# A trunk layer with 16 experts: router chain reordered, expert columns gathered directly, output projection tile by tile

## The chip, the cores and the metric

One core of a Trainium2 chip runs the whole kernel. The metric is device time in microseconds of one execution; the figure for a kernel is the median of its runs, and a profile is one further execution.

## The reference

One layer over 384 tokens of width 1024: 128 context tokens and 256 latent ones (`T` = 3 tiles of 128).

```
h   = LN0(x) * (1 + scale1) + shift1
x   = LN1(alpha * x + gate1 * (merged @ w_out))       # merged: two mixing branches, each projected and gated
h2  = LN0(x) * (1 + scale2) + shift2
aff = softmax(h2 @ w_router)                          # 16 experts, context and latent tokens apart
gate, idx = top_k(aff.T, cap)                         # each expert takes 16 context and 32 latent tokens
xe  = h2[idx];  hid = silu(xe @ w_gate) * (xe @ w_up) # per expert 1024 x 2816, twice
out[idx] += (hid @ w_down) * gate                     # 2816 x 1024
x   = LN2(alpha * x + gate2 * out)
```

All in fp32. The expert weights are 34.6 MB for each of the 16 experts.

## The kernel before

Semaphores and the order in each engine's program are written out by hand. Tiles of 128 tokens come in `ORDER` (1, 2, 0): latent, latent, context.

*Projections.* Every weight matrix comes in chunks of 512 columns (2 MB, `WCHUNKS`; 16 and 17 are `pa`, 18 and 19 `pb`, 20 and 21 the output projection `wo`). A chunk is split into a rounded part (ScalarE, `split_high`) and a rest (VectorE, `split`); a job of PE (`job`, L740) makes one 128 x 512 result from three products over 8 k-tiles, so 24 matmuls, into PSUM bank 0 or 1, and waits until the result of the job before the last is copied. Chunks alternate between two pairs of slots at the top of the ring: one pair is free when the chunk two before has been used. A `pa` or `pb` result is multiplied by its gate and added to `merged`; a `wo` result is multiplied by the gate row `g1b` and added to alpha * x (L1396, L1397). Six `wo` jobs, in order (tile, half) = (0,0), (1,0), (0,1), (1,1), (2,0), (2,1). Merged tiles are turned by PE (L696) before they are used.

*Between.* VectorE makes both layer norms of a tile (`layer_norms`: statistics L1363, affine L1370 and L1372, first part of h2 L1705); ScalarE scales (L1314) and GpSimd adds the shift (L670) for the first two tiles, VectorE does all of it for the third. h2 lies row by row. PE turns it, ScalarE copies it, PE makes the router logits (L966), softmax follows, the probabilities are turned and copied to SBUF, and VectorE finds the best 8 at a time (`best`, L1717 to L1721): four rounds for latent, two for context tokens. The slots go to DRAM and back, to be broadcast to 128 partitions (L677, L679). The selection of expert 0 is made another way, from a turned comparison (L1757, L1004, L1759). The broadcasts of rows (gate, scale, shift, norms) are DMAs on GpSimd's queue; `bc_loaded` counts ten.

*Experts.* Per expert PE gathers the 64 rows by a one-hot product (L1021, 512 wide), ScalarE copies, PE turns them (L1026), VectorE copies, then gate and up (L1038, 192 instructions in the trace), the turn of the hidden part (L1046), down (L1060), the combination (L1068), which VectorE adds to x (L1794). SyncE's queue loads the weights into a ring of six quarters (gate and up in 4 quarters of 2.88 MB each, down in 4 groups): the first two quarters after the merged tiles are copied, the next after the last `wo` copy, all later ones when PE has used what lay there (`gate_used`, `up_used`, `down_used`).

## Time and profile before

| | |
|---|---|
| median of 3 runs | 1866.29 us (1866.17 to 1867.25) |
| profiled execution | 1867.64 us, of which the span is 1865.8 |
| granted TensorE clock, mean | 0.97 of full speed |
| busy: PE, PEld, DVE, ACT, POOL | 1672.9, 799.4, 503.0, 338.3, 46.3 us |
| read from HBM | 637.8 MB, mean 344 GB/s |

A span runs from the first instruction to the last. The projections end at 543 us, the experts begin at 574 us and fill the rest. PE's busy time is not PE at its peak, and a share of the whole span says nothing of one stage; the stages are read one by one below.

### The profile page before, as it was taken

Reading aid. Unit: us, or ns where it says so; the run is one execution under the profiler, and the core shown is the slowest. Engines: PE = TensorE matmul, PEld = TensorE weight load, DVE = VectorE, ACT = ScalarE, POOL = GpSimd, SP = SyncE. Lnnn points to the kernel's source line nnn. Section 1 sums busy time; section 2 is a strip of 40 time slices with the busy share of each in tenths; the row PEclk is TensorE's granted clock in tenths of the full one; section 3 lists DMA queues with packets and bytes.
Section 4 is the critical chain, followed back from the end, with each engine's and each line's share of the span. In section 5 each row is a group of like instructions: output and inputs, shape, how many; then the busy total and the mean of one; then the engine's idle time right before and its main releaser. Section 6 shows DMA issues by size and latency. Waiting matters only on the chain.

```text
span 1865.8 us, 18738 instructions
## 1 busy us (share of the span) xinstructions
PE 1672.9 (90%) x7753; PEld 799.4 (43%) x7753; DVE 503.0 (27%) x956; ACT 338.3 (18%) x663; POOL 46.3 (2%) x71
## 2 busy tenths in 40 slices
PE   5999999999977998998988999798998989999896
PEld 2767787778763333333333323233333323333232
DVE  5385547775672101011010101101011010101102
ACT  2443355553321000000000000000000000000000
POOL 2001000010010000000000000000000000000000
PEclk9999999999988999999999999999999999999998
DMA  9683343325559999999999999999999999999994
GB/s 355 219 278 98 110 125 90 91 76 182 188 201 376 431 431 429 432 428 431 433 429 430 431 430 430 431 433 428 428 433 429 431 431 431 429 431 429 431 432 184
DMA packets 60569, 642.04 MB, mean 344 GB/s; under 512 B 6142, under 2 KB 6286, under 8 KB 32878
## 3 DMA queue, kind: packets, MB, share of 16 engines
q1 hardware_dynamic: 56464, 629.96, 81.6%
q0 software_dynamic: 4064, 11.54, 1.9%
q8 instruction: 26, 0.43, 0.1%
q14 instruction: 15, 0.12, 0.0%
HBM read 637.77 MB, written 3.71 MB: 344 GB/s over the span
## 4 chain that ended last, share of the span: by engine, by line
PE 67%; DMA 22%; DVE 7%; ACT 2%; issue 2%; POOL 0%; SPq 0%; DVEq 0%; ACTq 0%; POOLq 0%
PE banks L1038 24%; DMA ring<-in_w_exp_down 16%; PE banks L740 15%; PE banks L1060 11%; PE banks L1068 4%; DMA ring<-in_w_exp_up 4%; PE banks L1021 2%; PE banks L738 2%; PE banks L696 1%; PE banks L755 1%; DMA ring<-in_w_in 1%; PE banks L896 1%; DVE O L1786 1%; PE banks L1026 1%; DMA O<-in_ln_b 1%
## 5 line engine op out<-in xcount | busy, mean ns | idle before, releaser
L1038 PE MATMUL banks<-ring,O 128*64 128x512 f32 (+1 forms) x3072 | 641.5, 576 | 27.6 <-DMA ring<-in_w_exp_up 13.8
L1038 PEld LDWEIGHTS banks<-ring,O 128*64 128x64 f32 x3072 | 219.6, 134 | 441.3 <-issue 414.3
L1060 PE MATMUL banks<-ring,O 128*64 128x512 f32 x1408 | 328.3, 623 | 25.1 <-DMA ring<-in_w_exp_down 15.0
L1060 PEld LDWEIGHTS banks<-ring,O 128*64 128x64 f32 x1408 | 101.6, 144 | 242.0 <-issue 195.3
L1781 DVE TENSOR_TENSOR O<-O,banks 128x512 f32<-128x512 f32 (+1 forms) x48 | 28.0, 639 | 650.3 <-PE banks L1038 650.3
L740 PE MATMUL banks<-slot_parts,X_parts 128*128 128x512 f32 x672 | 183.4, 403 | 0.0
L740 PEld LDWEIGHTS banks<-slot_parts,X_parts 128*128 128x128 f32 x672 | 121.3, 188 | 39.5 <-issue 11.0
L1786 DVE TENSOR_TENSOR O<-banks,O 128x512 f32<-128x512 f32 x32 | 20.6, 687 | 390.1 <-PE banks L1060 390.1
L740 PE MATMUL banks<-slot_parts,H_parts 128*128 128x512 f32 x432 | 115.7, 396 | 0.4 <-DVE X L1397 0.4
L1463 DVE TENSOR_TENSOR slot_parts<-ring,slot_parts 128x512 fp32r<-128x512 f32 x176 | 110.2, 687 | 16.6 <-ACT slot_parts L1107 15.8
L1068 PE MATMUL banks<-O 128*128 128x512 f32 x192 | 86.6, 601 | 22.4 <-DVE O L1786 22.4
L1330 ACT ACTIVATE O<-banks 128x512 f32<-128x512 f32 x16 | 9.6, 597 | 469.8 <-PE banks L1021 469.8
L740 PEld LDWEIGHTS banks<-slot_parts,H_parts 128*128 128x128 f32 x432 | 82.0, 191 | 17.9 <-DVE X L1397 0.9
L1336 ACT ACTIVATE O<-banks 128x512 f32<-128x512 f32 (+1 forms) x48 | 24.3, 559 | 355.0 <-PE banks L1046 354.8
L1107 ACT ACTIVATE slot_parts<-ring 128x512 fp32r<-128x512 f32 x144 | 77.8, 620 | 56.2 <-DMA ring<-in_w_proj_b 19.1
L1333 ACT ACTIVATE O<-banks 128x512 f32<-128x512 f32 (+1 forms) x48 | 23.5, 562 | 327.6 <-PE banks L1038 327.6
L1794 DVE TENSOR_TENSOR X<-X,banks 128x512 f32<-128x512 f32 x90 | 61.8, 687 | 31.1 <-PE banks L1068 31.1
L1068 PEld LDWEIGHTS banks<-O 128*128 128x128 f32 x192 | 35.2, 190 | 74.7 <-issue 40.6
L1021 PE MATMUL banks<-O 128*64 128x512 f32 x192 | 46.1, 617 | 12.4 <-DVE X L1794 11.8
L1046 PE MATMUL banks<-kf,O 128*128 128x128 f32 x176 | 28.4, 315 | 31.1 <-DVE O L1781 31.1
L696 PE MATMUL banks<-kf,O 128*128 128x128 f32 x144 | 26.6, 315 | 23.0 <-DVE O L1421 11.2
L1046 PEld LDWEIGHTS banks<-kf,O 128*128 128x128 f32 x176 | 24.3, 214 | 42.4 <-DVE O L1781 42.4
(252 smaller groups left out, 1070.7 us busy)
## 6 DMA issues: line engine op xcount, KB each, us to landing
ring<-in_w_exp_gate SPq DMA_DIRECT2D x64, 2816.0 KB, 30.6
ring<-in_w_exp_up SPq DMA_DIRECT2D x64, 2816.0 KB, 26.1
ring<-in_w_exp_down SPq DMA_DIRECT2D x32, 3072.0 KB, 23.5
ring<-in_w_exp_down SPq DMA_DIRECT2D x16, 4096.0 KB, 28.0
ring<-in_w_in SPq DMA_DIRECT2D x16, 2048.0 KB, 9.9
ring<-in_w_mod SPq DMA_DIRECT2D x16, 1024.0 KB, 10.8
ring<-in_w_exp_down SPq DMA_DIRECT2D x16, 1024.0 KB, 32.3
O<-in_w_mod SPq DMA_DIRECT2D x8, 1024.0 KB, 5.3
```

What stands on the lines that cost most here:

```text
L696: x = pe.transpose(banks[:, 2 + b % 2, i * P:(i + 1) * P], src, ident)
L738: x = pe.matmul(out[:, 0:NT], w[:, k, i * P:(i + 1) * P], a[:, k, :], **flags)
L740: x = pe.matmul(out, a[:, k, i * P:(i + 1) * P], w[:, k, :], **flags)
L1021: x = pe.matmul(banks[64 * w:64 * w + 64, 3, :], sel[:, t, :], h2_half(t, w), start=(t == 0), stop=(t == T - 1))
L1038: x = pe.matmul(banks[64 * w:64 * w + 64, 3 * m + b, 0:(i1 - i0) * P], xeT[:, k % 4, 64 * (k // 4):64 * (k // 4) + 64], w4[:, kk, w, i0 * ...
L1046: x = pe.transpose(banks[:, b, (i - i0) * P:(i - i0 + 1) * P], hid_cols[:, i, :], ident)
L1060: x = pe.matmul(banks[64 * w:64 * w + 64, 6 + dc, :], hidT[:, i, 64 * w:64 * w + 64], wd[:, i, w, dc * BANK:(dc + 1) * BANK], start=(i == ...
L1068: pe.matmul(banks[:, 2 * t + dc, :], selT[:, t * P:(t + 1) * P], yrow[:, dc * BANK:(dc + 1) * BANK], start=not last, stop=True, skip_group ...
L1107: return act.activation(out, in_, ACT.Copy, scale=scale)
L1463: dve.tensor_tensor(low[:, k, :], w[:, k, :], high[:, k, :].bitcast(F32), ALU.subtract).then_inc(w_split, 1)
L1786: dve.tensor_tensor(yrow[:, cs], banks[:, 6 + dc, :], g2s[:, cs], ALU.mult).then_inc(y_cp, 1)
L1794: dve.tensor_tensor(dst, dst, banks[:, n, :], ALU.add).then_inc(acc_done, 1)
```

## The change

Five edits. (1) The output projection goes tile by tile; its first chunk has a place of its own below the slots, loaded once `pa` is done, and its second one takes the slots of the first `pb` chunk. The reload of x goes ahead of the `pb` chunks; scale2 is incremented beside `pb`; the last three broadcast rows have a semaphore of their own. (2) h2 is written chunk-wise, each k-tile's 128 columns together (column p * 8 + k of x goes to chunk k), from x, scale and shift read with a step of 8. ScalarE normalises from x, GpSimd multiplies and adds in halves. (3) The chain from h2 to the slots is interleaved, and the top-8 search reads the probabilities in PSUM. (4) Each expert's columns are gathered directly: 24 matmuls with a chunk of h2 as weights and the one-hot selection (32 or 16 slots, both in 32 columns) as moving data; the gathered rows and their turn are gone. (5) The slots are broadcast by PE, for expert 0 first, for all others between gate and up of expert 0, which is now outside the loop; the way by DRAM is gone, and the last norm's two rows are loaded after that broadcast.

```diff
+WO_FIRST, WO_SECOND = (CHUNK_OF["out", h * BANK] for h in range(2))
+PAIR = [n % 2 for n in range(WO_FIRST)] + [2, 0]
...
-WO_ORDER = [(0, 0), (1, 0), (0, 1), (1, 1), (2, 0), (2, 1)]
+WO_ORDER = [(n, h) for n in range(T) for h in range(2)]
...
+        def w_raw(n, k):
+            return wslot[2 * PAIR[n]][:, k, :] if PAIR[n] < 2 else reg(4 * UNIT + k * BANK, BANK)
+
+        def w_low(n, k):
+            if PAIR[n] < 2:
+                return wpart[2 * PAIR[n]][:, k, :]
+            return tile_of(E_r, k) if k < 6 else tile_of(spare_r, k - 6)
+
+        def w_high_of(n, k):
+            if PAIR[n] < 2:
+                return wpart[2 * PAIR[n] + 1][:, k, :]
+            return tile_of(spare_r, k + 2) if k < 2 else tile_of(C_r, k - 2)
...
+        h2_cols = O4[:].rearrange("p (t k n) -> p t k n", t=T, k=KT)
 
         def h2_half(t, w):
-            return h2[:, t, :].rearrange("p (n w k) -> p w n k", w=2, k=4)[:, w]
-
-        xeT = O3[:, BANK:2 * BANK].rearrange("p (i n) -> p i n", n=P)
+            return h2_cols[:, t, 4 * w:4 * w + 4, :]
+
+        def in_columns(row, w):
+            return row.rearrange("p (n k) -> p k n", k=KT)[:, 4 * w:4 * w + 4, :]
@@ sync
             def load_chunk(n):
                 if n < 2:
                     sp.wait_ge(mod0_used, 4 * n + 2)
+                elif n == WO_FIRST:
+                    sp.wait_ge(job_done, J_PA[-1] + 1)
                 else:
-                    sp.wait_ge(low_used, n - 1)
-                sp.dma_start(wslot[low_slot(n)], w_chunk(n)).then_inc(wsem[n % 2], 16)
+                    sp.wait_ge(low_used, before_in_pair(n)[-1] + 1)
+                dst = wslot[2 * PAIR[n]] if PAIR[n] < 2 else reg(4 * UNIT, KT * BANK).rearrange("p (k n) -> p k n", k=KT)
+                sp.dma_start(dst, w_chunk(n)).then_inc(wsem[PAIR[n]], 16)
...
-            for n in range(5, len(WCHUNKS)):
+            for n in range(5, CHUNK_OF["pb", 0]):
                 load_chunk(n)
-
             sp.wait_ge(job_done, J_GB[-1] + 1)
             sp.dma_start(x_r[:, 0, :], x_prompt[0]).then_inc(ld_x2, 16)
             sp.dma_start(x_r[:, 1:3, :], x_sample[0].rearrange("(t p) d -> p t d", p=P)).then_inc(ld_x2, 16)
+            for n in range(CHUNK_OF["pb", 0], len(WCHUNKS)):
+                load_chunk(n)
...
+            def load_quarter(m, q):
+                sp.dma_start(quarter((4 * m + q) % 6), gate_up(m, 0, q)).then_inc((land_g, land_u)[m][q], 16)
+
+            sp.wait_ge(job_done, J_PB[-1] + 1)
+            load_quarter(1, 1)
             wait_family(sp, F_M)
-            for q in range(4):
-                if q == 2:
-                    wait_job_copied(sp, J_WO[-1])
-                sp.dma_start(quarter(q), gate_up(0, 0, q)).then_inc(land_g[q], 16)
-            for q in range(4):
-                if q >= 2:
-                    sp.wait_ge(gate_used, q - 1)
-                sp.dma_start(quarter((4 + q) % 6), gate_up(1, 0, q)).then_inc(land_u[q], 16)
+            load_quarter(0, 0)
+            wait_job_copied(sp, J_WO[-1])
+            for q in range(1, 4):
+                load_quarter(0, q)
+            load_quarter(1, 0)
+            for q in range(2, 4):
+                sp.wait_ge(gate_used, q - 1)
+                load_quarter(1, q)
@@ gpsimd
             for g in range(2):
-                pool.dma_start(sh2b[:, g, :], mods[g, 3:4].to_broadcast((P, D))).then_inc(bc_loaded, 16)
-            pool.dma_start(l1b, ln1_b.to_broadcast((P, D))).then_inc(bc_loaded, 16)
+                pool.dma_start(sh2b[:, g, :], mods[g, 3:4].to_broadcast((P, D))).then_inc(bc_late, 16)
+            pool.dma_start(l1b, ln1_b.to_broadcast((P, D))).then_inc(bc_late, 16)
 
             for n in range(2):
                 t = ORDER[n]
-                if n == 0:
-                    pool.wait_ge(bc_loaded, 160)
+                g = min(t, 1)
                 pool.wait_ge(h2_norm, n + 1)
-                pool.tensor_tensor(h2[:, t, :], h2[:, t, :], sh2b[:, min(t, 1), :], ALU.add).then_inc(h2_ready[n], 1)
+                for w in range(2):
+                    dst = h2_half(t, w)
+                    pool.tensor_tensor(dst, dst, in_columns(sc2b[:, g, :], w), ALU.mult).then_inc(h2_scaled, 1)
+                    pool.wait_ge(h2_scaled, 2 * n + w + 1)
+                    pool.tensor_tensor(dst, dst, in_columns(sh2b[:, g, :], w), ALU.add).then_inc(h2_ready[n], 1)
 
             wait_job_copied(pool, J_WO[-1])
...
-            pool.wait_ge(rt_slots, 1)
-            pool.dma_start(slot_tokens, slots[:, 0:SLOT]).then_inc(rt_stored, 16)
-            pool.wait_ge(rt_stored, 16)
-            pool.dma_start(slot_bc, slot_tokens.rearrange("e s -> (e s)")[None].to_broadcast((P, NE * SLOT))).then_inc(rt_bc, 16)
-
-            pool.wait_ge(rt_tt, 1)
+            pool.wait_ge(rt_all, 1)
             pool.dma_start(l2g, ln2_g.to_broadcast((P, D))).then_inc(ld_end, 16)
             pool.dma_start(l2b, ln2_b.to_broadcast((P, D))).then_inc(ld_end, 16)
@@ tensor
+            for b in range(2):
+                logits(0, b)
+            for n in (1, 2):
+                for b in range(2):
+                    pe.wait_ge(h2_ready[n], b + 1)
+                    turn_half(h2, n, b)
+                    if n == 2 and b:
+                        turn_probs(0)
+                    logits(n, b)
             turn_probs(1)
-            logits(2)
             turn_probs(2)
+            wait_job_copied(pe, J_WO[-1])
+
+            def one_expert(e):
+
+                return ident[0:NE, e:e + 1].to_broadcast((NE, P))
+
+            def gather(k, ts):
+
+                s0 = k % 4 * SLOT + (LAT0 if ts[0] else CTX0)
+                for t in ts:
+                    x = pe.matmul(banks[:, 6 + k // 4, s0:s0 + CAP_L], h2_cols[:, t, k, :], sel[:, t, :],
+                                  start=(t == ts[0]), stop=(t == ts[-1]))
+                return x
+
+            pe.wait_ge(rt_lat, 1)
+            pe.matmul(banks[:, 1, 0:CAP_L], one_expert(0), slots[:, 0:CAP_L], start=True, stop=True).then_inc(rt_first, 1)
+            pe.wait_ge(sel_ready, 2)
+            for k in range(KT):
+                gather(k, (1, 2))
+            pe.wait_ge(rt_ctx, 1)
+            pe.matmul(banks[:, 1, CAP_L:SLOT], one_expert(0), slots[:, CAP_L:SLOT], start=True, stop=True).then_inc(rt_first, 1)
+            pe.wait_ge(sel_ready, 3)
+            for k in range(KT):
+                x = gather(k, (0,))
+            x.then_inc(xet_done, 1)
             pe.wait_ge(rt_slots, 2)
...
+            def broadcast_slots():
+
+                for e in range(NE):
+                    x = pe.matmul(banks[:, 6 + e // 8, e % 8 * SLOT:(e % 8 + 1) * SLOT], one_expert(e), slots[:, 0:SLOT],
+                                  start=True, stop=True)
+                x.then_inc(rt_all, 1)
...
+            def expert(e, first=False, last=False):
+
+                if not first:
+                    pe.wait_ge(sel_ready, e * T + T)
+                    for k in range(KT):
+                        gather(k, (1, 2))
+                        x = gather(k, (0,))
+                    x.then_inc(xet_done, 1)
+                pe.wait_ge(xet_cp, 2 * e + 2)
                 pe.wait_ge(acc_done, e * 6 + 6)
-                for t in range(T):
-                    for w in range(2):
-                        x = pe.matmul(banks[64 * w:64 * w + 64, 3, :], sel[:, t, :], h2_half(t, w),
-                                      start=(t == 0), stop=(t == T - 1))
-                x.then_inc(xe_done, 1)
-                pe.wait_ge(xe_cp, e + 1)
-                for i in range(4):
-                    x = pe.transpose(banks[:, 4, i * P:(i + 1) * P], xe_cols[:, i, :], ident)
-                x.then_inc(xet_done, 1)
-                pe.wait_ge(xet_cp, e + 1)
...
+                    if first and m == 0:
+                        broadcast_slots()
+                        pe.wait_ge(rt_cols, 2)
@@ scalar
+                act.wait_ge(x1_ready, n + 1)
+                act.activation(h2_cols[:, t], x_r[:, t, :].rearrange("p (n k) -> p k n", k=KT), ACT.Identity, scale=s("rstd", t, t + 1),
+                               bias=s("nmr", t, t + 1)).then_inc(h2_norm, 1)
+            for parity in range(2):
+                tile_copy(act, F_H2, 0, h2T, cp, parity)
             x1_dev(2, 0)
+            for parity in range(2):
+                tile_copy(act, F_H2, 1, h2T, cp, parity)
             x1_dev(2, 1)
+            router_exps(0)
+            for parity in range(2):
+                tile_copy(act, F_H2, 2, h2T, cp, parity)
+            router_exps(1)
+            router_exps(2)
+            act.wait_ge(h2_norm, 2)
+            times_alpha(0)
...
-            with act.Fori(0, NE) as e:
-                act.wait_ge(xe_done, e + 1)
-                act.activation(xe, banks[:, 3, :], ACT.Copy).then_inc(xe_cp, 1)
+            act.wait_ge(xet_done, 1)
+            cp(xeT[:, 0:4, :], banks[:, 6, 0:4 * SLOT].rearrange("p (k s) -> p k s", s=SLOT)).then_inc(xet_cp, 1)
+            act.wait_ge(rt_all, 1)
+            for w in range(2):
+                cp(slot_bc[:, 8 * w:8 * w + 8, :], banks[:, 6 + w, :].rearrange("p (e s) -> p e s", s=SLOT)).then_inc(rt_bc, 1)
@@ vector
             for n, j in enumerate(J_PB):
                 job_copy(j)
-                if 0 < n < T:
+                if n == 0:
+                    dve.wait_ge(bc_loaded, 112)
+                    for g in range(2):
+                        note(dve.tensor_scalar(sc2b[:, g, :], sc2b[:, g, :], 1.0, None, ALU.add))
+                elif n < T:
                     split(19, KT // 2 * (n - 1), KT // 2 * n)
-                if T <= n < T + 2:
-                    split(20, KT // 2 * (n - T), KT // 2 * (n - T + 1))
-            merged_low(0)
-            merged_low(1)
-            for k in range(0, KT, 2):
-                split(21, k, k + 2)
-            dve.wait_ge(bc_loaded, 160)
+                elif n == T:
+                    split(20)
+                else:
+                    merged_low(n - T - 1)
+                    split(21, KT // 2 * (n - T - 1), KT // 2 * (n - T))
             dve.wait_ge(ld_x2, 32)
-            for g in range(2):
-                note(dve.tensor_scalar(sc2b[:, g, :], sc2b[:, g, :], 1.0, None, ALU.add))
 
             def softmax_max(n):
                 t = ORDER[n]
...
-                if n == 2:
-                    softmax_max(1)
+                job_copy(between)
...
+                rstd(t)
+                dve.tensor_scalar(s("nmr", t, t + 1), s("mv", 2 * t, 2 * t + 1), s("rstd", t, t + 1), -1.0,
+                                  ALU.mult, ALU.mult).then_inc(x1_ready, 1)
...
             job_copy(J_WO[0])
+            merged_low(2)
             job_copy(J_WO[1])
-            merged_low(2)
-            job_copy(J_WO[2])
-            layer_norms(0)
+            dve.wait_ge(bc_late, 48)
+            layer_norms(0, J_WO[2])
             job_copy(J_WO[3])
-            layer_norms(1)
-            job_copy(J_WO[4])
-            softmax_max(0)
-            softmax_scale(0)
-            job_copy(J_WO[5])
-            layer_norms(2)
-            softmax_scale(1)
-            tile_copy(dve, F_H2, 2, h2T, dve.tensor_copy, 1)
-
+            layer_norms(1, J_WO[4])
             note(dve.memset(slots, -1.0))
             note(dve.memset(gates, 0.0))
-            turned_probs(0)
-            turned_probs(1)
-            best(SEQ, NT, LAT0, CAP_L)
+
+            t = ORDER[2]
+            half_stats(t, 0)
+            job_copy(J_WO[5])
+            stats(t, ws=(1,)).then_inc(x1_var[0], 1)
+            dve.wait_ge(x1_std[0], 3)
+            rstd(t)
+            link(affine(x_r, t, l1g, l1b))
+            stats(t).then_inc(x1_var[1], 1)
+            softmax_max(0)
+            dve.wait_ge(x1_std[1], 3)
+            rstd(t)
+            g = min(t, 1)
+            for w in range(2):
+                dst = h2_half(t, w)
+                link(dve.scalar_tensor_tensor(out=dst, in0=in_columns(x_r[:, t, :], w), scalar=s("mv", 2 * t, 2 * t + 1),
+                                              in1=in_columns(sc2b[:, g, :], w), op0=ALU.subtract, op1=ALU.mult))
+                dve.scalar_tensor_tensor(out=dst, in0=dst, scalar=s("rstd", t, t + 1), in1=in_columns(sh2b[:, g, :], w),
+                                         op0=ALU.mult, op1=ALU.add).then_inc(h2_ready[2], 1)
+            softmax_scale(0)
+            softmax_max(1)
+            softmax_scale(1)
+            dve.wait_ge(rt_tr, 2)
+            best(lat_probs, LAT0, 0, CAP_L // 8)
             softmax_max(2)
+            best(lat_probs, LAT0, 1, CAP_L // 8)
             softmax_scale(2)
-            turned_probs(2)
-            best(0, SEQ, CTX0, CAP_C)
-            settle()
-            note(dve.tensor_scalar(slots[:, LAT0:LAT0 + CAP_L], idxu[:, LAT0:LAT0 + CAP_L], float(SEQ), None, ALU.add))
-            link(dve.tensor_copy(slots[:, CTX0:CTX0 + CAP_C], idxu[:, CTX0:CTX0 + CAP_C]))
+            best(lat_probs, LAT0, 2, CAP_L // 8)
+            best(lat_probs, LAT0, 3, CAP_L // 8)
+            dve.tensor_scalar(slots[:, LAT0:LAT0 + CAP_L], idxu[:, LAT0:LAT0 + CAP_L], float(SEQ), None, ALU.add).then_inc(rt_lat, 1)
+            dve.wait_ge(rt_tr, 3)
+            best(context_probs, CTX0, 0, CAP_C // 8)
+
+            def first_selection(t):
+                s0 = LAT0 if t else CTX0
+                dve.tensor_scalar(sel[:, t, :], banks[:, 1, s0:s0 + CAP_L], iota_c[:, t:t + 1], None, ALU.is_equal).then_inc(sel_ready, 1)
+
+            dve.wait_ge(rt_first, 1)
+            first_selection(1)
+            first_selection(2)
+            best(context_probs, CTX0, 1, CAP_C // 8)
+            dve.tensor_copy(slots[:, CTX0:CTX0 + CAP_C], idxu[:, CTX0:CTX0 + CAP_C]).then_inc(rt_ctx, 1)
+            dve.wait_ge(rt_first, 2)
+            first_selection(0)
+            dve.wait_ge(rt_lat, 1)
+            dve.wait_ge(rt_ctx, 1)
             dve.tensor_copy(slots[:, SLOT:2 * SLOT], slots[:, 0:SLOT]).then_inc(rt_slots, 1)
             dve.tensor_copy(gates[:, SLOT:2 * SLOT], gates[:, 0:SLOT]).then_inc(rt_slots, 1)
+            dve.wait_ge(xet_done, 1)
+            dve.tensor_copy(xeT[:, 4:8, :], banks[:, 7, 0:4 * SLOT].rearrange("p (k s) -> p k s", s=SLOT)).then_inc(xet_cp, 1)
```

## Rows read from the trace of the kernel before

**Rows 1.** The page's part 2: GB/s moved, in 40 equal slices.

```profile
GB/s 355 219 278 98 110 125 90 91 76 182 188 201 376 431 431 429 432 428 431 433 429 430 431 430 430 431 433 428 428 433 429 431 431 431 429 431 429 431 432 184
```

**Rows 2.** The chain of waits in time order: start us, length us, what.

```profile
501.65 11.69 DMA O<-in_ln_b
...
842.50 28.15 DMA ring<-in_w_exp_down
```

**Rows 3.** Windows: stretch and its length, busy us per engine, PEclk, DMA share, GB/s.

```profile
540.00:545.00 5.00, 5.00 (x31) 4.33 (x29) 4.22 (x7) 1.90 (x3) 0.38 (x1) 1.00 0.00 0
...
560.00:565.00 5.00, 4.26 (x21) 4.03 (x19) 3.91 (x15) 0.60 (x1) 0.00 (x0) 0.50 0.93 347
...
585.00:590.00 5.00, 5.00 (x26) 1.64 (x24) 0.00 (x0) 0.00 (x0) 0.00 (x0) 1.00 0.63 221
...
640.00:720.00 80.00, 73.60 (x339) 25.59 (x337) 8.74 (x16) 6.10 (x9) 0.00 (x0) 1.00 1.01 430
```

**Rows 4.** Timeline of SyncE's queue: start us, us, line, DMA, times.

```profile
549.83 41.58 SPq L571 DMA_DIRECT2D ring<-in_w_exp_up  x4
601.03 10.75 SPq L559 DMA_DIRECT2D ring<-in_w_exp_down  x4
...
678.72 10.94 SPq L559 DMA_DIRECT2D ring<-in_w_exp_down  x4
```

**Rows 5.** Timeline of all engines, projections to router, same columns and idle time before.

```profile
493.81 1.03 PE L696 MATMUL banks<-kf,ring 128*128 128x128 f32 x8
...
505.83 4.91 DVE L1463 TENSOR_TENSOR slot_parts<-ring,slot_parts 128x512 fp32r<-128x512 f32 x8 [0.62 <-ACT slot_parts L1107]
...
514.57 0.69 DVE L1396 TENSOR_TENSOR ring<-banks,O 128x512 f32<-128x512 f32 x1
...
525.28 5.60 PE L740 MATMUL banks<-slot_parts,H_parts 128*128 128x512 f32 x24
...
541.35 1.99 PE L740 MATMUL banks<-slot_parts,oaT_low 128*128 128x512 f32 x8
...
543.17 1.85 PE L966 MATMUL banks<-O,H 128*128 128x16 f32 x16
...
557.51 1.28 DVE L1372 SCALAR_TENSOR_TENSOR O<-O,sm 128x1024 f32<-128x1024 f32 x1
...
560.83 3.43 PE L966 MATMUL banks<-O,H 128*128 128x16 f32 x16
```

**Rows 6.** The same timeline, up to the first gate matmul.

```profile
574.37 4.20 PE L1021 MATMUL banks<-O 128*64 128x512 f32 x12 [0.60 <-DVE O L1759]
...
578.60 0.53 POOL L682 DMA_DIRECT2D O<-in_ln_g  x1
...
580.88 40.01 PE L1038 MATMUL banks<-ring,O 128*64 128x512 f32 x192 [0.86 <-DVE O L1772]
```

**Rows 7.** The same timeline in the third expert: gather, first gate matmuls.

```profile
729.54 2.79 PE L1021 MATMUL banks<-O 128*64 128x512 f32 x12 [0.78 <-DVE X L1794]
...
734.64 5.62 PE L1038 MATMUL banks<-ring,O 128*64 128x512 f32 x26 [0.86 <-DVE O L1772]
```

**Rows 8.** Single lines: duration ns min/median/max, first and last start us, form.

```profile
L1626 DVE TENSOR_TENSOR O<-O,ring x3: 1212/1214/2934, 401.4 to 405.4; 128x1024 f32<-128x1024 f32 x3
...
L1046 PEld LDWEIGHTS banks<-kf,O x165: 197/213/231, 622.8 to 1739.3; 128*128 128x128 f32 x165
...
L696 PEld LDWEIGHTS banks<-kf,ring x8: 138/140/140, 493.6 to 494.5; 128*128 128x128 f32 x8
```

**Rows 9.** Groups of instructions: form, count | busy us, mean ns | idle before.

```profile
L1717 DVE MAX8 O<-O 16x8 f32<-16x256 f32 x4 | 1.7, 416 | 0.1
...
L670 POOL TENSOR_TENSOR O<-O 128x1024 f32<-128x1024 f32 x2 | 4.7, 2340 | 40.1 <-ACT O L1314 40.1
```

**Rows 10.** DMA queues: packets, MB, busy share of 16 engines' span.

```profile
q1 hardware_dynamic: 56464, 629.96, 81.6%
q0 software_dynamic: 4064, 11.54, 1.9%
```

234 lines of the change are left out of this document (108 added, 126 removed).

## The prediction

> **What bounds the kernel now.** I read the 40 slices of the page first. From slice 13 on the core moves some 430 GB/s: the sixteen experts stream their weights [rows 1]. The chain of waits names PE for the first three experts, and from 842.50 us on a DMA of down weights in nearly every expert [rows 2]. Both are one state: the DMA engines are never idle (share 1.01 at 430 GB/s from 640 to 720) while PE first eats the lead it has [rows 3]. An expert is 34.6 MB, so 80.3 us at 431 GB/s; PE's own cycle is 76.1 us (gather to gather). The end therefore hangs on when the stream of expert 0 runs without a gap, plus every byte that is added after that. Before that point the queue is idle twice: 0 GB/s from 540 to 545, share 0.63 from 585 to 590 [rows 3]. SyncE's own row tells why: six quarters of 2.88 MB fit in the ring, four of them issued after the last output projection copy (549 us), and the seventh waits until PE has used the first. The last real gap ends with the down weights at 601.03, issued when all four gate quarters are used, 20.15 us after PE's first gate matmul at 580.88 [rows 4, 6]. **So the end moves one for one with that first gate matmul**, and I cost the change by it.
>
> **Part 1: output projection.** Before, DVE stands until 513.36 for the last broadcast row (11.69 us in the chain) [rows 2], copies its first tile at 514.57, and PE's last output matmul ends at 541.35+1.98 = 543.3 [rows 5]. The broadcasts are issued when the last pb job is done, just before 501.65. After, sc2b's add needs only the seven early rows and goes beside the first pb job; the three late rows are waited for after two output jobs. W_out's first half is loaded outside the slots when pa is done, its split lies beside pb, and the second half gets the slot of pb's first half, so both are there by about 490. PE can then run: one turn of merged tile 1 (8 transposes, 1.03), six jobs of 24 matmuls at 5.45 (the row shows 5.60 for 24 with its overlap), a second turn 1.0 [rows 5]: 500.1 + 34.7 = 534.8. Gain 8.5. DVE beside it: per job 1.45 of copies (2 x 0.69 and a gap), merged rests 1.3, splits of 0.61 a piece (4.91 for 8 [rows 5]), 4 to 8 of them; all below 5.45 but for one job, and PE may be one job behind. The late rows are 1.5 MB beside 2.9 MB of up weights now issued at the same moment: 10 us at full rate, so 511 to 513, needed at 514. Cost 0, up to 3 if it is late. SyncE's queue: x is reloaded before the pb weights; it stands behind the second pa chunk only, and delays nothing that is needed before 450; I take 0, up to 3.
>
> **Part 2: from the last output job to the third tile of h2.** Before, 543.3 to 557.51+1.28 = 558.8 [rows 5]: 15.5, because DVE was still busy with the second tile. After, DVE on the third tile: copy 1.45, second half of the statistics 0.9, root and reciprocal 0.65, affine 2 x 1.3, statistics 1.5, 0.65, four half-width operations at 0.69 = 2.8 (widths of 512 take 0.69 and of 1024 1.28 [rows 5]). Sum 10.5, so 545.3: 13.5 earlier, if nothing is in the way. Two things are.
>
> *GpSimd.* Before it does one 1024-wide add per tile, 2.34 [rows 9]; after, four 512-wide ones, some 1.25 each with start and wait, 5.4 per tile. They now fall beside DVE's affine operations on the next tile. The trace has one such meeting: DVE's product of two SBUF operands took 2.93 once, beside a GpSimd operation, and 1.21 twice without [rows 8]: it stood still till GpSimd was done. Tile 1's affine begins about 527.5 with GpSimd at work until 529.2, tile 2's about 538.9 with GpSimd from 536.2. Alternating, each pair costs DVE 1.5 and then 2.5 more: 3.7 in all after what PE hides; R (third tile ready) = 549. Bounds 0 and 3.7. By the Trainium skill ("SBUF — State Buffer", Who interferes with whom) a VectorE operation with two SBUF inputs and a GpSimd one that reads SBUF exclude each other for a whole instruction; the row agrees, and by it the upper bound would be the value.
>
> *Steps of 8 elements.* h2 is now written chunk by chunk, so x, scale and shift are read with a step of 32 bytes by ACT (1.15 per tile), GpSimd and DVE. No row shows this on these engines. The nearest: PE's weight load of a tile with a step of 44 bytes took 213 ns, a contiguous one 140 [rows 8]: 73 ns more for 128 elements. If DVE's four halves take 1.2 instead of 0.69, that is +2.1; ACT +0.9; GpSimd's operations 1.9 instead of 1.25, which through the exclusion and through ACT (it turns tile 1 before it takes tile 2's root) adds 3.7. R = 555.7. Bounds 0 and 6.7; a gain I exclude, since the same elements are read. The row shows a half of a doubling, so I take the half: R = 552.3, **6.5 earlier**. The Trainium skill ("Advanced Engine Details and Errata", Memory Cachelines) says accesses that go to another 16-byte line each time are penalised; by that alone R would be 555.7. The weight-load row is in line with it.
>
> **Part 3: from h2 to the first gate matmul.** Before: 558.8 to 580.88 = 22.1 [rows 5, 6]. After, from R: 4 transposes 1.05 at half clock, copy 0.65, four logit matmuls at 0.43 (3.43 for 8) 1.7, softmax scale and turn; top-8 rounds start at R+4.0 rather than +3.5. Four latent rounds of 1.48 (a MAX8 is 0.42 [rows 9]; PSUM as source I take as equal) with the context's softmax between, 6.3, so latent slots at R+10.3. Then a broadcast matmul 0.4, a context round 1.1 and two selections 0.4 (DVE), and 16 gather matmuls of 128 weights by 32 columns. Nearest row: the logits, 16 columns, 0.25 each at full clock (1.85 + 0.2 for 8), 0.43 at half [rows 5, 6]. PE does little after 535 and stands at half clock (granted 0.50 from 560 to 565, at 1.2 GHz, in spite of 5 us of transposes and logits) [rows 3]. 16 cost 4.0 to 6.9, I take 6.2; second broadcast and selection 0.7; 8 more 2.0 to 3.4, I take 2.0; copy 0.5. First gate matmul R+21.2; lower bound 19.1, upper 24.9 (all at half and the first 3 us of gate too). **0.9 earlier.** What goes is the DRAM round trip of the slots, the selection turn and the six 512-wide gathers with their turn (574.37 to 580.88).
>
> **Part 4: what comes after.** (a) ln2's two rows (1.05 MB) were issued at 578.6 [rows 6], where the queue ran dry; now they wait for the slot broadcast after expert 0's gate part, in the full stream. By the queues' rows, 2.4 us per MB on the hardware queue, 3.1 on the software queue [rows 10]: 2.5 to 3.3, **+2.8**. (b) 16 broadcast matmuls, 4.0, now stand between gate and up of expert 0. The first down piece and ln2's rows keep the DMA busy for them. Expert 1's down weights are issued at 678.72 [rows 4], 2.5 before the queue would run dry; PE is 4.0+0.75 later by then, the queue 2.8: **+0.3** at most 1. (c) Every later expert: 24 small matmuls at 0.25 = 6.0 and a copy 0.6 against the 5.1 from 729.54 to 734.64 [rows 7] and 0.8 waited for DVE's sums: +0.75 on 76.1, under the 80.3 of the stream: 0. (d) The tail is the same.
>
> **Sum**, against the profiled execution's 1867.64 (span 1865.8 and 1.84 around it): -6.5 - 0.9 + 2.8 + 0.3 = -4.3, so 1863.3; the median of the runs is 1.35 below that execution, so **1862.0**.
>
> **Rivals.** *A, nothing is in the way*: R = 545.3 to 546.5 and a clock that rises early: -12.5 - 3 + 2.8 = -12; with part of it, 1856. For it: both prices of part 2 are inferred. Against: rows 8. *B, no change*: steps and exclusion in full, R = 555.7: -3.1 - 0.9 + 3.1 = -1, 1865.5. For it: both of rows 8. *C, slower by PE*: the gather of each expert costs over 9.4 (5.1 + 4.3 of slack), as it would at half clock (24 x 0.43 = 10.3 and a copy): PE's cycle becomes 81.9, over 80.3 by 1.6, over 14 experts with the lead used up: 1885 less the start's gain, 1880; it decides from 0.37 us per matmul on. Against: PE is busy right before each gather and the clock is 1.00 there. *D*, the late sides together (second pa chunk or late rows +3, gather at half clock +3.7, R = 555.7): 1870.
>
> **Chances.** Forecast 0.48 (own range 1859 to 1865), A 0.20, B 0.20, C 0.04, D 0.08. The measurement tells 0.2%, 3.7 us, from no change. Under 1862.6 lie A and six tenths of the forecast with the rest of its low side: 0.51; slower C and most of D: 0.11; within: 0.38. Range 1855.5 to 1869.5.
>
> **What would show it.** Right: no DVE wait for ln_b; output matmuls end near 535; the four quarters issued near 538; third tile of h2 near 552; first gate matmul near 573.5 and down weights 20 us later; stream at 430 GB/s from there; DVE's affine operations longer than 1.3 where GpSimd is at work; half-width ones above 0.69. Wrong: first gate matmul before 568 or after 578; DMA share below 0.98 after expert 0; a per-expert cycle that differs from 80.3.

## The result, and the profile after

The changed kernel takes **1884.95 us** (median of 4 runs, 1881.69 to 1893.35), the kernel before 1866.62 (4 runs, 1866.17 to 1867.25): ratio 1.0105, interval 1.007 to 1.014. Faster was forecast, and it is slower by 18 us. The runs lie 12 us apart, those of before 1. The profiled execution is the lowest of the four, 1881.69 with a span of 1879.9.

The page after: busy time of PE, the granted clock and the GB/s in 40 slices, the shares of the chain, and two of the groups.

```profile
PE 1751.5 (93%) x8298; PEld 888.3 (47%) x8298; DVE 497.9 (26%) x952; ACT 296.9 (16%) x633; POOL 55.1 (3%) x75
...
PEclk8999999999977999999989898988999999999998
...
GB/s 357 226 285 88 96 126 93 84 90 236 223 243 243 423 404 426 430 430 430 434 428 432 429 430 430 429 432 427 416 424 423 414 432 430 429 430 431 431 432 153
...
PE 89%; DVE 6%; issue 2%; DMA 2%; ACT 1%; POOL 0%; SPq 0%; DVEq 0%; ACTq 0%
...
L1096 PE MATMUL banks<-ring,O 128*64 128x512 f32 (+1 forms) x3072 | 673.3, 600 | 10.4 <-DVE O L1868 10.2
...
L1043 PE MATMUL banks<-O 128*128 128x32 f32 x768 | 101.2, 296 | 1.1 <-DVE O L1838 1.1
```

The chain of waits before gave PE 67% and DMA 22%; now DMA has 2%. The stream of weights no longer sets the end, TensorE does. It shows in the GB/s: 404, 416, 414 in slices where before had 428 and more [rows 1]. Gate and up products, unchanged in kind, take 600 ns on average (L1096) instead of 576 (L1038 of before).

SyncE's queue, and PE from the router to expert 0's up part, with one wait of VectorE:

```profile
535.92 1.28 SPq L590 DMA_DIRECT2D ring<-in_w_exp_gate  x3
...
598.23 17.80 SPq L585 DMA_DIRECT2D ring<-in_w_exp_down  x4
620.37 24.60 SPq L613 DMA_DIRECT2D ring<-in_w_exp_gate  x4
```

```profile
514.63 1.29 DVE L1438 BATCH_NORM_STATS2 sm<-X 128x6 f32<-128x512 f32 x2 [1.12 <-DMA O<-in_ln_b]
...
527.89 2.54 DVE L1456 SCALAR_TENSOR_TENSOR X<-X,sm,O 128x1024 f32<-128x1024 f32 x1
...
549.84 1.15 DVE L1820 SCALAR_TENSOR_TENSOR O<-O,sm 128x512 f32<-128x512 f32 x1
...
563.78 7.04 PE L1043 MATMUL banks<-O 128*128 128x32 f32 x32 [0.74 <-DVE O L1838]
...
571.72 3.62 PE L1043 MATMUL banks<-O 128*128 128x32 f32 x16 [0.34 <-DVE O L1838]
...
575.86 22.32 PE L1096 MATMUL banks<-ring,O 128*64 128x512 f32 x96 [0.20 <-DVE O L1852]
598.12 4.43 PE L1065 MATMUL banks<-O,kf 16*128 16x64 f32 x32
602.47 22.65 PE L1096 MATMUL banks<-ring,O 128*64 128x512 f32 x96
```

The front is as forecast: quarters at 535.9, third tile of h2 at 549.84 + 1.15 = 551.0 (forecast 552.3), first gate product at 575.86 (573.5; before 580.88 [rows 6]). A product of f32 stands as two records, so 16 products of the gather are x32. From there the lead of 5 us is lost. PE's timeline at the gather of expert 6, and the windows around it (columns as in [rows 3]):

```profile
1055.11 7.24 PE L1043 MATMUL banks<-O 128*128 128x32 f32 x48
1063.04 22.41 PE L1096 MATMUL banks<-ring,O 128*64 128x512 f32 x94 [0.69 <-DVE O L1868]
```

```profile
1050.00:1054.00 4.00, 4.00 (x10) 1.85 (x11) 2.46 (x4) 0.00 (x0) 0.00 (x0) 1.00 1.00 428
1054.00:1058.00 4.00, 4.00 (x30) 3.28 (x29) 1.65 (x3) 0.00 (x0) 0.00 (x0) 1.00 0.96 411
1058.00:1062.00 4.00, 4.00 (x23) 4.00 (x22) 0.00 (x0) 0.00 (x0) 0.00 (x0) 0.56 1.00 428
1062.00:1066.00 4.00, 3.31 (x10) 1.22 (x11) 1.25 (x5) 0.39 (x1) 0.00 (x0) 0.50 1.05 451
1066.00:1070.00 4.00, 4.00 (x14) 1.16 (x12) 0.00 (x0) 0.00 (x0) 0.00 (x0) 0.66 1.01 434
```

PE is busy in every microsecond from 1050 to 1062, and yet the granted clock goes from 1.00 (2.4 GHz) to 0.50 (1.2 GHz) inside the 48 records; in windows of one microsecond it is 1.00 up to 1058, 0.72 in the next and 0.50 from 1059 on. PEld (the weight loads) fills the time there: 4.00 of 4.00. The gate part begins at the low level.

The fall comes inside the gather in 7 of the 15 experts after the first. In the other 8 the gather runs through at 1.00, in 5.44 us, and the clock falls as it ends or less than 1 us later, so that only the gate part is slow. Expert 2 is one of these (gather from 738.26 to 743.70):

```profile
738.00:744.00 6.00, 5.71 (x49) 5.36 (x48) 1.24 (x3) 0.26 (x1) 0.00 (x0) 1.00 1.03 437
744.00:748.00 4.00, 3.60 (x10) 1.15 (x12) 0.99 (x5) 0.13 (x1) 0.00 (x0) 0.57 0.97 417
```

**Where 14.1 us of span come from**, by starts of rows: first gate product 5.0 earlier; from there to expert 1's gather 82.2 instead of 72.6, +9.6 (gate 22.3 for 20.2, broadcast 4.4, up 22.6 for 19.9, down 22.0 for 20.7, less 1.0 between combine and gather); 14 cycles of 80.4 instead of 79.9, +7.6; tail +1.9. Cycles of 80.4 on average are not the stream's pace here: from one combine to the next the trace gives 80.2, 79.0, 78.7, 78.6, 80.6, 82.2, 82.0, 83.7, 82.0, 82.0, 80.2, 78.8, 78.8, 78.6. Their length goes with the clock (third column from the right), here for the shortest, a middle one and the longest:

```profile
890.72:969.31 78.59, 73.87 (x351) 29.41 (x352) 8.41 (x16) 3.54 (x7) 0.00 (x0) 0.96 1.00 430
1049.89:1132.08 82.19, 77.35 (x352) 31.25 (x352) 8.41 (x16) 3.32 (x7) 0.00 (x0) 0.92 1.00 430
1214.12:1297.81 83.69, 78.85 (x351) 31.97 (x352) 8.41 (x16) 3.32 (x7) 0.00 (x0) 0.90 1.00 429
```

In the kernel before, the mean of a cycle is 0.96 to 1.00. It too falls to 0.50 at times, near the turn of the hidden part; its row gathers after the first all run at 1.00. The changed kernel has both falls.

### The profile page after: what moved, and what is told of

Read it like the earlier page. It is cut to its first block, busy times and chain, and to the rows that moved or that the text cites. A ratio compares the mean times of both kernels' runs of the same rounds, so it can differ in the third digit from the quotient of the medians.

```text
span 1879.9 us, 19789 instructions
## 1 busy us (share of the span) xinstructions
PE 1751.5 (93%) x8298; PEld 888.3 (47%) x8298; DVE 497.9 (26%) x952; ACT 296.9 (16%) x633; POOL 55.1 (3%) x75
## 4 chain that ended last, share of the span: by engine, by line
PE 89%; DVE 6%; issue 2%; DMA 2%; ACT 1%; POOL 0%; SPq 0%; DVEq 0%; ACTq 0%
PE banks L1096 36%; PE banks L1123 17%; PE banks L771 16%; PE banks L1043 5%; PE banks L1131 4%; PE banks L769 2%; PE banks L1107 1%; PE banks L725 1%; DVE O L1880 1%; PE banks L786 1%; DMA ring<-in_w_in 1%; PE banks L927 1%; DVE O L1885 1%; PE banks L883 1%; PE banks L948 1%
## 5 line engine op out<-in xcount | busy, mean ns | idle before, releaser
L1096 PE MATMUL banks<-ring,O 128*64 128x512 f32 (+1 forms) x3072 | 673.3, 600 | 10.4 <-DVE O L1868 10.2
L1096 PEld LDWEIGHTS banks<-ring,O 128*64 128x64 f32 x3072 | 222.0, 141 | 451.6 <-issue 450.6
L1123 PEld LDWEIGHTS banks<-ring,O 128*64 128x64 f32 x1408 | 103.3, 145 | 225.5 <-issue 211.6
L1546 DVE TENSOR_TENSOR slot_parts<-ring,slot_parts 128x512 fp32r<-128x512 f32 x168 | 105.2, 685 | 14.9 <-ACT slot_parts L1171 14.2
L1043 PEld LDWEIGHTS banks<-O 128*128 128x128 f32 x768 | 101.9, 216 | 8.5 <-issue 7.2
L771 PE MATMUL banks<-slot_parts,H_parts 128*128 128x512 f32 x384 | 102.3, 390 | 0.0
L1043 PE MATMUL banks<-O 128*128 128x32 f32 x768 | 101.2, 296 | 1.1 <-DVE O L1838 1.1
L1412 ACT ACTIVATE O<-banks 128x256 f32<-128x256 f32 x15 | 5.8, 385 | 501.5 <-PE banks L1043 501.5
L1171 ACT ACTIVATE slot_parts<-ring 128x512 fp32r<-128x512 f32 x136 | 73.5, 619 | 49.5 <-DMA ring<-in_w_proj_b 20.6
L771 PEld LDWEIGHTS banks<-slot_parts,H_parts 128*128 128x128 f32 x384 | 72.1, 188 | 14.9
L1131 PEld LDWEIGHTS banks<-O 128*128 128x128 f32 x192 | 35.2, 190 | 75.7 <-issue 75.7
L1107 PE MATMUL banks<-kf,O 128*128 128x128 f32 x176 | 30.5, 332 | 31.2 <-DVE O L1880 31.2
```

Source lines behind the costliest of these rows:

```text
L771: x = pe.matmul(out, a[:, k, i * P:(i + 1) * P], w, **flags)
L1043: x = pe.matmul(banks[:, 6 + k // 4, s0:s0 + CAP_L], h2_cols[:, t, k, :], sel[:, t, :], start=(t == ts[0]), stop=(t == ts[-1]))
L1096: x = pe.matmul(banks[64 * w:64 * w + 64, 3 * m + b, 0:(i1 - i0) * P], xeT[:, k, :], w4[:, kk, w, i0 * P:i1 * P], start=(k == 0), stop=(k ...
L1107: x = pe.transpose(banks[:, b, (i - i0) * P:(i - i0 + 1) * P], hid_cols[:, i, :], ident)
L1123: x = pe.matmul(banks[64 * w:64 * w + 64, 6 + dc, :], hidT[:, i, 64 * w:64 * w + 64], wd[:, i, w, dc * BANK:(dc + 1) * BANK], start=(i == ...
L1131: pe.matmul(banks[:, 2 * t + dc, :], selT[:, t * P:(t + 1) * P], yrow[:, dc * BANK:(dc + 1) * BANK], start=not last, stop=True, skip_group ...
```

## The experiments

Theory 1: the run of small products lowers TensorE's granted clock, and TensorE's cycle passes the stream's. Theory 2: the broadcast between gate and up costs the stream. Theory 3: the late broadcast rows race the first expert load. Each ratio is against runs of the kernel before on the same chip; the chips differ between groups (median of before 1866.44 beside e1 to e4, 1865.21 beside e5 to e8, 1865.95 beside e9 to e11, 1866.10 beside e12 and e13). "e1" and so on are short for the labels in order.

### e1, e2: the gather in other forms

```
e1:  experts 1 to 15
-    24 x matmul(h2_cols[:, t, k], sel[:, t])        # 32 columns
+    6 x matmul(sel[:, t], h2_half(t, w)); ScalarE copy; 4 transposes; one copy
e2:  for i in steps of the down part:
+        if 0 < i <= 8: three column products of expert e + 1 into bank 3
         4 down products
```

> The changed kernel, with the selection of experts 1 to 15 made as before the change: six products of 128x512 into a row image, ScalarE's copy, four turns, one copy. Expert 0 keeps the direct columns, and all else stays. Theory 1 (the 24 small products of an expert's gather last 5.3 to 7.4 us, TensorE's granted clock falls to half in them and stays there into the gate part, so the cycle is TensorE's 80.4 us instead of the stream's 79.9): the cycle of the experts falls back to 79.9 us, the dips to 0.50 around the gather shorten to what before had, the run takes 1864 to 1869 us. Rival 1 (the loss of 14 to 18 us sits in expert 0 and in what is loaded late there, or in the strides of h2): it stays at 1878 or more.

> The changed kernel, with the 24 column products of the next expert put between the 44 down products of the current one, three ahead of each step of four, into bank 3, and one ScalarE copy of the 512 columns while the down part runs. Theory 1: the small products no longer stand in one run, their weight loads lie beside wide products, the clock stays at 1.00 except around the hidden part, TensorE's work on an expert falls to 74 to 78 us, under the stream's 79.9: 1863 to 1869 us, and SyncE is what the waits name again. Rival 1 (as for e1): 1878 or more. Rival 2 (any small product costs its two loads, 0.2 to 0.3 us, wherever it stands, and pulls the clock down there too): TensorE's work stays over 80 us, 1880 or more.

**e1: 1870.47** (8 runs, 1866.58 to 1874.85), 1.0023 [1.0012, 1.0033]. 14.5 us of the 18.3 are gone with this edit alone; the mean clock is 0.971 (changed kernel 0.939), the chain gives DMA 21%. That is just over the range expected of theory 1 and far under the rival's 1878. Theory 1 holds for the main part, but 4 us stay.

**e2: 1876.80** (5 runs), 1.005 [1.0035, 1.0065]. A miss in time (1863 to 1869 expected), right on the clock. PE in the down part of e2, and its clock:

```profile
1029.62 0.85 PE L1070 MATMUL banks<-O 128*128 128x32 f32 x6
1030.40 1.94 PE L1132 MATMUL banks<-ring,O 128*64 128x512 f32 x8
1032.27 0.85 PE L1070 MATMUL banks<-O 128*128 128x32 f32 x6
```

```profile
1030.00:1035.00 5.00, 5.00 (x28) 2.15 (x27) 0.00 (x0) 0.00 (x0) 0.00 (x0) 1.00 0.95 406
1035.00:1040.00 5.00, 5.00 (x28) 2.38 (x28) 0.00 (x0) 0.00 (x0) 0.00 (x0) 1.00 0.96 406
```

The clock stays at 1.00 with the small products between wide ones. But three small ones still take 0.79 us (1029.62 to 1030.40 and so on), 6.3 for 24: nothing is hidden. The cycle is 78.5 us for PE alone in the first five experts, too near the stream's 80.4 to absorb a dip. VectorE also waited 6.5 us for the late rows in this execution.

### e3, e4, e7: the kernel before with products added

```
 wait_ge(acc_done, e * 6 + 6)
+e3: for i in range(24): matmul(banks[:, 0, 0:32], <128x128 of h2>, sel[:, t, 0:32])
+e4: for i in range(12): matmul(banks[:, 0, :], ident, <128x512 of h2>)
+e7: for i in range(6):  the same as e4
```

> The kernel before, with 24 more products of 128x128 by 32 columns ahead of each expert's row gather, their results unused. At full clock they are 24 x 0.22 = 5.3 us; 76.1 + 5.3 = 81.4 us against the stream's 79.9 gives 15 x 1.5 = 22 us, about 1889 us. Theory 1 adds the clock: the 24 take up to 7.4 us and the gate part some 2 us more, 84 to 86 us a cycle, 1925 to 1955 us. Rival (length only, no effect of kind): 1885 to 1895 us, as e4.

> The kernel before, with 12 more products of 128x128 by 512 columns in the same place, results unused: 12 x 0.45 = 5.4 us, the same TensorE time as in e3 at full clock. Theory 1: no dip of the clock beyond those of before, 81.5 us a cycle, 1885 to 1895 us, 40 us or more under e3. Rival (length only): the same time as e3 within 5 us.

> The kernel before with 6 more products of 128x128 by 512 columns ahead of each row gather, results unused. The wide products of e4 had 2 records each of 0.44 us, 10.6 us in all; 6 are 5.3 us, the time that e3's 24 small ones take at full clock. TensorE's own cycle from the rows is 75.8 + 5.3 = 81.1 us. Theory 1: 81.1 plus the 1.2 to 1.5 us that the dips of before cost (e4: 87.2 measured, 86.4 by rows), 82.3 to 82.9 us a cycle, some 1905 to 1915 us, against e3's 85.9 us a cycle and 1970 us. Rival (only length counts): e3's time.

**e3: 1970.51** (4 runs); **e4: 1989.83** (4 runs); **e7: 1909.49** (5 runs, 1905.41 to 1918.84), 1.0227 [1.021, 1.0244]. e4 was mis-sized: I had read a record as a product, so its 12 were 10.6 us and not 5.4. e7 is the fair partner of e3, and came as expected; e3 came 15 us over its range. First e3, then e7, PE ahead of the row gather (L1023):

```profile
1003.92 6.53 PE L1020 MATMUL banks<-O 128*128 128x32 f32 x48 [0.78 <-DVE X L1796]
1010.37 5.11 PE L1023 MATMUL banks<-O 128*64 128x512 f32 x12
...
1088.58 5.92 PE L1020 MATMUL banks<-O 128*128 128x32 f32 x48 [0.78 <-DVE X L1796]
1094.43 4.05 PE L1023 MATMUL banks<-O 128*64 128x512 f32 x12
```

```profile
1075.76 5.42 PE L1020 MATMUL banks<-O,kf 128*128 128x512 f32 x12 [0.78 <-DVE X L1796]
1081.10 2.79 PE L1023 MATMUL banks<-O 128*64 128x512 f32 x12
...
1159.91 5.42 PE L1020 MATMUL banks<-O,kf 128*128 128x512 f32 x12 [0.78 <-DVE X L1796]
1165.25 2.79 PE L1023 MATMUL banks<-O 128*64 128x512 f32 x12
```

Behind wide products the row gather takes 2.79, as in [rows 7]; behind small ones 4.05 and 5.11. In the 15 experts after the first the clock is 1.00 through all of e7's added products and falls within all of e3's. The same TensorE time at full clock costs 44 us in one kind and 104 in the other (medians less those of before beside them): 60 us over 16 experts, 3.7 each. This is theory 1 measured alone, in a kernel that is otherwise the one before, and the rival (length only) is out.

### e5, e6, e8: expert 0 and the router, on e1

```
e5:  gate; up;
+    broadcast_slots()                 # was between gate and up
e6:  router
+    fill(n): n x matmul(banks[:, 0, 0:256], ident, kf[:, 0:256]) in TensorE's gaps, 21 in all
e8:  e5 + e6, and
-    16 x matmul(16x128, 16x64)
+    2 x matmul(ones, diagonal image of the slots, 512 columns)
```

> e1 with the 16 broadcast products of expert 0 moved from between its gate and up parts to behind the up part, where TensorE waits 1.9 us for the hidden part anyway. In e1 they take 4.9 us, expert 0's up products start that much later, and the last three down loads and the gate loads of expert 1 are issued 4 to 5 us later after the first one than before the change (22.1 us against 15.1 us). Theory 2 (the stream's start is not the issue of expert 0's first down group but the up part that frees the ring, so the broadcast costs the stream): 3 to 5 us under e1. Rival (the stream's start is the first down issue, as forecast, or expert 0's whole TensorE time, which only falls by 2): 0 to 2 us under e1.

> e1 with unused products of 128x128 by 256 columns in TensorE's gaps between 538 and 565 us, while the router waits for other engines (21 of them, 0.44 us each at full clock). Theory 1, for the start (the gather of expert 0 takes 10.7 us instead of 5.3 and the gate part 22 instead of 20.2 because the granted clock is 0.50 from 541 to 579 us): the clock stays at 1.00 at least up to 565 us, the first gate product comes 3 to 6 us earlier, the run is 2 to 6 us under e1. Rival (the small products pull the clock down whatever comes before, and the fillers are in the way): first gate product at 577 to 580 us, run as e1 or up to 3 us over it.

> e1 with the broadcast behind the up part and made of two products of 16x128 by 512 columns on a diagonal image (1.8 us instead of 4.9, inside the 1.9 us wait), and with the fillers of e6. If theories 1 and 2 hold, their gains add: 5 to 10 us under e1, 1858 to 1864 us, faster than both kernels. If only theory 2 holds: 1864 to 1867 us.

**e5: 1872.94** (6 runs), **e6: 1869.45** (10 runs, 1861.94 to 1872.71), **e8: 1868.34** (10 runs, 1863.38 to 1873.65), ratio of e8 1.0016 [1.0003, 1.0028]. None reached its gain, and the spreads of 7 to 11 us cover what they may have. Against its own runs of before e5 is 7.7 us slower, where e1 was 4.0. e5 leaves theory 2 open, with a sign against it: from the first gate product to the last combine the profiled executions of e1 and e5 take the same 1271.8 us. The traces say more. The profiles of e5 and e8 caught the late rows; in e8:

```profile
520.16 1.29 DVE L1465 BATCH_NORM_STATS2 sm<-X 128x6 f32<-128x512 f32 x2 [7.42 <-DMA O<-in_ln_b]
```

e6 waited 0.97 us at the same place. And the fillers of e8 did hold the clock at 1.00, up to the start of the gather:

```profile
560.00:565.00 5.00, 3.85 (x18) 2.73 (x16) 4.66 (x19) 3.20 (x5) 0.00 (x0) 1.00 0.96 328
565.00:570.00 5.00, 3.14 (x16) 3.03 (x16) 2.75 (x15) 0.00 (x0) 0.00 (x0) 0.75 1.02 426
570.00:575.00 5.00, 4.70 (x22) 4.50 (x21) 0.26 (x2) 0.00 (x0) 0.00 (x0) 0.50 1.01 433
```

```profile
567.26 6.88 PE L1060 MATMUL banks<-O 128*128 128x32 f32 x32 [1.02 <-DVE O L1865]
```

The clock is 1.00 from 566 to 567, 0.73 in the next microsecond and 0.50 after that. The gather's first product is at 567.26, so its products are hardly the cause here; PE had been busy for 0.40 of the 2.39 us before it. What the rows do show is the price of a column gather at 0.50: 6.88 + 3.62 us. It was the next thing to replace.

### e9, e11: all gathers by rows; e10, e12, e13: the first expert load held

```
e10: -    load_quarter(1, 1)
     +    sp.wait_ge(bc_late, 48); load_quarter(1, 1)
e12, e13: the same on e1, on e8
e9:  e13, expert 0: -  24 column products
                    +  4 row products on latent slots, 2 on context slots, copy, 4 transposes, copy
e11: e9 without fill()
```

> e8 with two more edits. First, expert 0 is gathered by rows too (four products of 512 columns once the latent slots are known, two once the context slots are, ScalarE's copy, four turns, one copy) on a selection zeroed beforehand: in e8 the fillers held the granted clock at 1.00 up to 566 us, and it fell to 0.50 inside the 32 small products of expert 0's gather (6.9 us for them, 3.6 for the next 16, and the gate part began at half clock). Second, SyncE waits for the three late broadcast rows before it issues the first expert load: in the profiles of e2, e5 and e8 these rows landed at 520 us, in those of the changed kernel, e1 and e6 at 513 to 515, and VectorE waited 7.4 us for them instead of 1 us. Theory 1 and theory 3 (that race of two queues is what spreads the runs of all these kernels over 8 to 12 us): first gate product 4 to 6 us earlier than in e8's good case, clock up through it, runs within 3 us of one another, median 1856 to 1861 us. Rival (the stream alone sets the end, whatever expert 0 does): 1865 us or more.

> The changed kernel with one edit: SyncE waits for the three late broadcast rows before it issues the first expert load. Theory 3: VectorE's wait for them is 0 to 1.2 us in every run, the runs that lost 6 to 7 us there fall away, median 1881 to 1883 us and a narrow spread. Theory 1 alone (the spread of 1882 to 1893 us comes from where the dips of the clock fall): median 1885 us and the old spread.

> e9 without the fillers. The clock is then 0.50 from some 541 us on whatever the gather does. Theory 1: expert 0's row gather is 2 to 3 us longer than in e9 and the gate part starts at half clock, 22 us instead of 20.2: 3 to 5 us over e9. Rival (the fillers do nothing, the shape of the gather is all): as e9 within 1 us.

> e1 with SyncE's first expert load held until the three late broadcast rows have landed. Theory 3 (e1 loses 6 to 7 us in the runs in which those rows land at 520 us instead of 513): median 1866 to 1868 us instead of e1's 1870.5, spread under 5 us. Rival (the spread of e1 is of another origin, as e10 suggests for the changed kernel, whose runs stayed at 1875 and 1892): median 1870 us, spread 8 us as before.

> e8 with the same hold, which is e9 but for expert 0's gather: direct columns here, rows there. Theory 3: 3 to 4 us under e8's 1868.3, some 1864 to 1865 us. Theory 1: e9 stays 4 to 6 us below it (5 us of gather and 2 us of gate part at half clock). Rival to theory 1: e9's gain is all from the hold, and this run takes 1858 to 1860 us.

| kernel | median us (runs) | range | ratio [interval] |
|---|---|---|---|
| e9 | **1858.94** (5) | 1856.03 to 1861.21 | 0.9959 [0.9947, 0.9972] |
| e10 | 1884.43 (6) | 1874.93 to 1892.86 | 1.0105 [1.0071, 1.0138] |
| e11 | 1863.03 (11) | 1860.32 to 1868.03 | 0.9985 [0.9977, 0.9994] |
| e12 | 1868.30 (11) | 1866.12 to 1871.44 | 1.0015 [1.0006, 1.0024] |
| e13 | 1867.09 (12) | 1862.84 to 1874.03 | 1.0006 [0.9994, 1.0018] |

**e9 beats both kernels**, by 7 us the one before. PE in e9, from expert 0's gather on, and the windows there:

```profile
563.30 2.85 PE L1063 MATMUL banks<-O 128*64 128x512 f32 x8 [1.02 <-DVE O L1865]
...
567.06 1.98 PE L1063 MATMUL banks<-O 128*64 128x512 f32 x4 [0.34 <-DVE O L1865]
...
571.70 41.26 PE L1118 MATMUL banks<-ring,O 128*64 128x512 f32 x192 [0.53 <-DVE O L1879]
612.90 1.98 PE L1089 MATMUL banks<-O,cT 16*128 16x512 f32 x4
```

```profile
565.00:570.00 5.00, 3.96 (x11) 1.06 (x8) 0.44 (x3) 0.90 (x2) 0.00 (x0) 0.50 0.79 338
570.00:575.00 5.00, 4.47 (x16) 1.82 (x17) 2.44 (x6) 0.98 (x1) 0.00 (x0) 0.56 0.00 0
575.00:580.00 5.00, 5.00 (x26) 1.66 (x24) 0.00 (x0) 0.00 (x0) 0.00 (x0) 1.00 0.27 72
```

First gate product at 571.70, 9.2 before that of the kernel before; gate and up 41.3 without a stop; the broadcast is 2.0 behind them. The expected "clock up through it" did not come: the clock falls to 0.50 in the row gather too, at 564, with its wide products, and is back at 1.00 only behind the start of the gate part. The row gather is cheaper here since it is short (2.85 + 1.98), not since it keeps the clock. The last combine starts at 1841.36 against 1847.74. From e13 to e9 only the form of expert 0's gather changes: 8.2 us (8.0 when each is set against its own runs of before), more than the 4 to 6 expected (first gate product 575.91 there, so 4.2 of it by that row; the rest was not separated). e9 against e11: the fillers are worth 4.1 by the medians, of which the rows show 1.3 at the first gate product (572.96 in e11).

**Theory 3** holds in the traces (VectorE doesn't wait for those rows in the profiles of e9 to e13) and is small in time: e12 is 2.2 us under e1, e13 1.3 under e8 (1.8 and 2.1 against their own runs of before), both less than the spread; e13 missed its 1864 to 1865. It does not explain the changed kernel: e10 stayed at 1884.43, as theory 1 alone had it, its runs in two groups, 1874.93 to 1877.08 and 1891.78 to 1892.86, with clocks 0.945 and 0.935. The cycles inside one trace wander between 78.4 and 83.7 us in e10 too. Within one execution of the changed kernel the long cycles are those with the lower clock (above). I read the two groups of e10 in the same way, as more or fewer of the long falls; no run controlled where they fall, so it stays an inference.

## Why the prediction was wrong

**What bounds (the stream) and the rule "one for one with the first gate product".** The stream bounds the kernel before, and in e9 the direction holds: 9.2 us earlier there, 6.4 at the last combine. One for one it does not hold, even where the later experts are gathered by rows. Three rows of e13:

```profile
575.91 42.16 PE L1120 MATMUL banks<-ring,O 128*64 128x512 f32 x192 [0.20 <-DVE O L1880]
598.22 10.75 SPq L591 DMA_DIRECT2D ring<-in_w_exp_down  x4
1848.05 5.39 PE L1156 MATMUL banks<-O 128*128 128x512 f32 x12 [1.48 <-DVE O L1922]
```

Its first gate product comes 5.0 us before that of the kernel before, its first down weights are issued only 2.8 earlier (before: 601.03), since the gate part starts at 0.50, and its last combine is 0.3 later (before: 1847.74). The prediction added ln2's rows for 2.8 us (part 4 (a)); that would be about the rest, but no run isolates it. For the changed kernel the rule holds only while TensorE's cycle stays under the stream's, and the prediction gave that condition its own rival. Of the 23 us between forecast and median, e1 gives back 14.5; the other 8.5 are left for what comes ahead of expert 1 and for this rule, and are not divided further.

**Part 1.** Output jobs end near 533.8 (534.8 forecast). VectorE waited 1.12 for ln_b; forecast was 0, up to 3. The bound was too tight: in the profiled executions of e2, e8 and e5 it is 6.5, 7.4 and 8.1. The 1.5 MB of rows are issued at the same moment as 2.9 MB on another queue (from 498.89 and at 498.62 in e8); where SyncE holds that load back (e9 to e13) the wait is gone. Why it is short in some executions without the hold was not found.

**Part 2.** Right. R is 551.0 against 552.3. Both obstacles exist: the affine took 2.54 and 2.42 beside GpSimd and 1.28 otherwise (by the Trainium skill, "SBUF — State Buffer", Who interferes with whom, they exclude each other; the trace agrees), and a half-width operation on step-8 data took 1.15 instead of 0.69, close to the 1.2 of which I had counted half; less of it reached the path than my sum had. What set R in the end was the way through ScalarE that the sum had named: VectorE stood 3.39 us, until 546.17, for the third tile's root.

**Part 3.** The term that missed is the gather of expert 0: 6.2 + 2.0 forecast, 7.04 + 3.62 measured, all at 0.50. First gate product 2.4 late, 3.7 counted from R: 24.9 where the sum had 21.2 (its terms add up to 21.6).

**Part 4 (b).** Priced +0.3 by expert 1's down issue alone. The stop holds back all of expert 0's up part, so the last down loads end their issue 17.8 us after the first instead of 10.75 and expert 1's gate loads are issued at 620.37 instead of 616.13. e9 removes it with other things; its own price was not isolated (e5).

**Part 4 (a) and (d).** ln2's rows were issued at 602.84 as forecast; their price was not measured. The tail is 1.9 us longer.

**Part 4 (c) is the step that failed**: "+0.75 on 76.1, under the 80.3 of the stream: 0". The length was right, even generous. At full clock, from the start of the combine to the first gate product, the changed kernel needs 5.22 + 5.44 (the gather in 8 of 15 experts) + 0.69 = 11.4 us, the one before 5.42 + 0.78 + 3.50 + 1.61 = 11.3 (the rows of e7 without the added six show it whole); gate, up, hidden part and down take 64.6 in e7's cycles at full clock, so PE's cycle is 75.9 to 76.0 in both. What the step left out is the clock. It costs the changed kernel 80.4 - 75.9 = 4.5 us an expert and the one before 0.2 to 1.7 (76.1 to 77.6 while PE-bound).

Rival C had the direction and the time (1880 forecast, 1881.69 profiled), but the time by luck. Its condition was a gather at half clock, from 0.37 us a product on; the gathers in the loop take 5.44 to 7.60 us, 0.23 to 0.32 a product, so by its own threshold nothing would have been lost. Most of the loss stands behind the gather: from the first gate product to the turn of the hidden part 43.2 to 44.6 us instead of 42.0. And its cycle of 81.9 leaves out the 0.8 of waiting that (c) counts off; with it, it is 81.1. Rival C got 0.04 for one reason, "PE is busy right before each gather and the clock is 1.00 there": that took the clock on entry for the clock during the run and behind it. [Rows 3] already had a hint, 0.50 from 560 to 565 with PE busy for 4.26 of 5 us and PEld for 4.03, though PE's waits around that stretch leave it a hint only.

The Trainium skill ("TensorE: Matmul & The Clock Gate", HAM oscillation) lays such falls to waits between bursts of matmuls. The rows of 1050 to 1062 differ: PE's last idle time, 1.48 us, ended at 1049.89, and the clock falls at 1058 with none in between; the measurement decides. A busy share read off a profile does not vouch for the clock.
